# Output projection of a conv and pool hybrid layer: six products in token chunks of 512, 512 and 8 in place of three of 344

## What is computed

```python
def trunk(x, c, conv_bufs, pool_bufs, start, w_ada, b_ada, g_norm, w_in, w_dw, b_dw,
          ln_g, ln_b, w_a_out, w_grp, pool_scale, w_b_out, w_out, g_final):
...
        m = jax.nn.sigmoid(proj[..., o5:o6]) * y_a + jax.nn.sigmoid(proj[..., o6:]) * y_b
        x = x + gate * (m @ w_out[l])
...
    return rms_norm(x, g_final), jnp.stack(new_conv), jnp.stack(new_pool)
```

## Time and profile before

| | |
|---|---|
| median of three executions | 1007.66 us |
| span of the profiled execution (first to last instruction) | 1007.2 us |
| TensorE busy in it | 977.5 us, 97% |
| VectorE busy in it | 694.8 us, 69% |
| ScalarE busy in it | 253.0 us, 25% |
| mean granted TensorE clock | 0.992 of full speed |

### The profile page before, as it was taken

How to read it: one execution, slowest core, us unless ns; L and a number is a source line. 1 busy time by engine, 2 the same in 40 slices (tenths; PEclk the granted TensorE clock), 3 DMA queues, 4 the chain that set the end, 5 groups by cost and what they waited for, 6 DMA issues and landing times.

```text
span 1007.2 us, 14744 instructions
## 1 busy us (share of the span) xinstructions
PE 977.5 (97%) x6196; PEld 962.9 (96%) x6196; DVE 694.8 (69%) x687; ACT 253.0 (25%) x264; POOL 1.9 (0%) x12
## 2 busy tenths in 40 slices
PE   4999999999999989999998999999999999999997
PEld 3799999999999979999998999999999998999996
DVE  6878987718898752889864489987879744343346
ACT  5541112121111221111211111122724512122241
POOL 0000000000000000000000000000000000000000
PEclk9999999999999999999999999999999999999998
DMA  9511221231230240122024112213871173124104
GB/s 379 234 43 63 93 72 53 84 121 42 84 116 27 74 143 22 63 84 96 27 75 142 42 42 106 79 53 106 331 283 40 40 315 126 42 85 189 42 1 169
DMA packets 31965, 106.46 MB, mean 106 GB/s; under 512 B 7713, under 2 KB 14113, under 8 KB 28449
## 3 DMA queue, kind: packets, MB, share of 16 engines
q1 hardware_dynamic: 28304, 92.82, 25.4%
q10 hardware_dynamic: 3600, 12.72, 3.2%
HBM read 82.74 MB, written 22.79 MB: 105 GB/s over the span
## 4 chain that ended last, share of the span: by engine, by line
PE 96%; DVE 1%; DMA 1%; issue 1%; ACT 1%; SPq 0%; DVEq 0%
PE ps L463 31%; PE ps L464 31%; PE ps L466 31%; DMA bf<-x_t 1%; PE aux L415 1%; DVE stage_hi L888 1%; PE ps L428 1%; PE aux L449 1%; PE aux L421 0%; PE aux L637 0%; DVE hf L1161 0%; ACT hf L712 0%; PE aux L629 0%; DVE bf L902 0%; ACT bf L706 0%
## 5 line engine op out<-in xcount | busy, mean ns | idle before, releaser
L464 PE MATMUL ps<-hr,w_hi 128*128 128x344 f32 x1536 | 488.3, 321 | 6.8 <-issue 6.8
L463 PE MATMUL ps<-hr,w_hi 128*128 128x344 f32 x1344 | 427.9, 321 | 2.2 <-ACT stage_hi L754 1.2
L930 DVE SCALAR_TENSOR_TENSOR conv_y<-conv_u,par,conv_y 128x1024 f32<-128x1024 f32 x240 | 308.1, 1284 | 20.6 <-PE ps L466 14.1
L464 PEld LDWEIGHTS ps<-hr,w_hi 128*128 128x128 f32 x1536 | 290.0, 189 | 7.3 <-issue 7.3
L466 PE MATMUL ps<-hr,w_lo 128*128 128x344 f32 x1344 | 286.0, 321 | 0.0
L463 PEld LDWEIGHTS ps<-hr,w_hi 128*128 128x128 f32 x1344 | 253.7, 189 | 4.5 <-issue 2.9
L466 PEld LDWEIGHTS ps<-hr,w_lo 128*128 128x128 f32 x1344 | 225.9, 189 | 0.0
L680 ACT ACTIVATE w_hi<-w_raw 128x1024 fp32r<-128x1024 f32 (+1 forms) x88 | 87.6, 996 | 274.3 <-PE ps L466 263.2
L864 DVE TENSOR_TENSOR w_lo<-w_raw,w_hi 128x1024 fp32r<-128x1024 f32 (+1 forms) x88 | 101.2, 1150 | 52.0 <-ACT w_hi L680 46.7
L463 PE MATMUL ps<-gr,w_hi 128*128 128x344 f32 x384 | 123.3, 323 | 0.0
L464 PE MATMUL ps<-gr,w_hi 128*128 128x344 f32 x384 | 121.8, 320 | 0.0
(11 more groups left out here) (128 smaller groups left out, 593.8 us busy)
## 6 DMA issues: line engine op xcount, KB each, us to landing
w_raw<-w_main SPq DMA_DIRECT2D x80, 512.0 KB, 3.3
ada_raw<-w_ada SPq DMA_DIRECT2D x8, 1024.0 KB, 16.8
bf<-x_t SPq DMA_DIRECT2D x4, 1032.0 KB, 8.0
sig_a<-stage_lo ACTq DMA_DIRECT2D x8, 516.0 KB, 2.7
sig_b<-stage_hi ACTq DMA_DIRECT2D x8, 516.0 KB, 2.6
y_conv<-conv_y SPq DMA_DIRECT2D x8, 516.0 KB, 3.0
silu_z<-stage_hi ACTq DMA_DIRECT2D x8, 516.0 KB, 4.0
bf<-y_conv SPq DMA_DIRECT2D x4, 1032.0 KB, 6.9
```

Of the source, the lines that this page charges most:

```text
L463: nc.tensor.matmul(out, wh, rhs_hi[:, cols(c)], start=(k == 0), stop=False)
L464: nc.tensor.matmul(out, wh, rhs_lo[:, cols(c)], start=False, stop=False)
L930: return v.scalar_tensor_tensor(out=y, in0=conv_u[:, x, k:k + SEQ], scalar=par[:, x, k:k + 1], in1=y, op0=ALU.mult, op1=ALU.add)
```

## The change

The first six products of the output projection are made by a new function, `wide_product`. Their token chunks are 512, 512 and 8 columns in place of three of 344, in the same three PSUM banks. The number of matmuls in a k step stays nine, and the columns that they stream stay 1032 in each of the three passes. The hardware loop of `job_pairs` is gone for these six. Since the first 1024 columns now fill two whole banks, VectorE makes the new x of the prompt in one instruction over both banks (`wide_x`) in place of three. The last two products and all that is before JOB_OUT are as they were.

```diff
+BANK = 512
+WIDE = [(0, 0, BANK), (1, BANK, SEQ), (2, SEQ, TOK)]
...
-            single(JOB_OUT, m_hi, m_lo, before_k=lambda k: pe.wait_ge(m_lo_done, k + 1))
-            job_pairs(JOB_OUT + 1, 4, m_hi, m_lo)
-            single(JOB_OUT + 5, m_hi, m_lo)
+
+            def wide_product(s):
+                pe.wait_ge(w_lo_done, s + 1)
+                pe.wait_ge(dve_evac, PAIRS * DVE_EVACS + s - 1 - JOB_B)
+                for k in range(KT):
+                    if s == JOB_OUT:
+                        pe.wait_ge(m_lo_done, k + 1)
+                    wh = w_hi[:, s % 2, k * P:(k + 1) * P]
+                    wl = w_lo[:, s % 2, k * P:(k + 1) * P]
+                    for bank, t0, t1 in WIDE:
+                        out = ps[:, s % 2, bank, 0:t1 - t0]
+                        nc.tensor.matmul(out, wh, m_hi[k][:, t0:t1], start=(k == 0), stop=False)
+                        nc.tensor.matmul(out, wh, m_lo[k][:, t0:t1], start=False, stop=False)
+                    for bank, t0, t1 in WIDE:
+                        last = nc.tensor.matmul(ps[:, s % 2, bank, 0:t1 - t0], wl, m_hi[k][:, t0:t1], start=False, stop=(k == KT - 1))
+                last.then_inc(pe_done, 1)
+
+            for s in range(JOB_OUT, JOB_OUT + 6):
+                wide_product(s)
...
+            def wide_x(m):
+                gate = mod[:, 4 + m // 4, m % 4, :]
+                product = ps[:, (JOB_OUT + m) % 2, :, :].rearrange("p c t -> p (c t)")
+                v.scalar_tensor_tensor(out=hf[:, KT + m, 0:SEQ], in0=product[:, 0:SEQ], scalar=gate[:, 0:1], in1=hf[:, m, 0:SEQ],
+                                       op0=ALU.mult, op1=ALU.add)
+                xs = hf[:, KT + m, SEQ:TOK]
+                link(v.tensor_tensor(xs, product[:, SEQ:TOK], gate[:, 1:NMOD], ALU.mult))
+                return v.tensor_tensor(xs, xs, hf[:, m, SEQ:TOK], ALU.add)
...
-                link(new_x(m, 0, CHUNKS))
+                link(wide_x(m))
```

## The result

The changed kernel takes 1021.03 us (median of 4 executions, 1020.29 to 1023.32), the kernel before 1007.73 (median of 4). The ratio is 1.0143 with a 95% interval of 1.0123 to 1.0162, so the change costs 14.4 us, between 12.4 and 16.3; the two medians lie 13.3 us apart. The forecast was 1021, with a range of 1014 to 1025.

What follows compares the result with a forecast made beforehand. TensorE's matmul stream was taken as the bound: a k step of 6 x 227.8 + 3 x 111 = 1700 ns in place of 1420, over 48 k steps +13.4 us on 1007.66, so 1021 us, range 1014 to 1025.

Steps and rivals of the forecast that it cites:

- What bounds the kernel: In the six products TensorE's stream never waits, so any nanosecond it gains or loses there is the kernel's; stretch 68.15 us.
- The short ones: Each 8-column matmul of the six products takes as long as its weight load, 111 ns, range 76 to 121.
- sign of being wrong: In the six products, records behind an 8-column matmul starting less than 70 ns apart, or doubled short matmuls, would refute the prediction.
- The long ones: Each 512-column matmul of the six products takes 227.8 ns, with 14.4 ns fixed per matmul; range 213.3 to 234.8.
- The loop, VectorE, the waits: In the six products, loop removal worth nothing, semaphore waits the same, VectorE's saving of 0.2 to 0.3 us a product hidden.
- Fully hidden loads: Rival: in the six products short matmuls cost only their columns, giving 1007.7 or 1001.4 us; 5% together with the skill's rule.
- A load at one cycle a column: Rival: fp32r weights in the six products load faster, a short matmul 67.7 ns, +7.2 us, 1014.9 us; 10%.
- Doubled short matmuls: Rival: each 8-column fp32r matmul of the six products runs as two, 222 ns, +29.4 us, 1037 us; 5%.
- The clock stayed at 1.00: Against the rival that the granted clock falls to 1.2 GHz in the six products, 1080 us or more; 2%.

Runs made afterwards that it cites:

- left out: Changed kernel without its 8-column matmuls, but for two in each product: 1005.47 us, ratio 1.000 to the kernel before.
- 120-column chunk: Changed kernel with chunks of 512, 400 and 120 columns in place of 512, 512 and 8: 1013.92 us, ratio 1.0077 to the kernel before.
- joined: Changed kernel with high by high and high by low of the sample columns as one 16-column matmul, VectorE adding the two: 1015.82 us, ratio 1.0110.
- three more: Changed kernel with low weights by the 8 sample columns run four times in place of once in each k step: 1037.54 us in one execution.
- grouped half weights: Changed kernel with the three 8-column matmuls of a k step in a row, most taking 64 of 128 weight columns: 1015.34 us, ratio 1.0098.
- half-weight runs: Changed kernel with most 8-column matmuls taking 64 of 128 weight columns: 1020.87 us, and 1015.34 us with the three of a k step in a row.
- written-out products alone: Changed kernel's code without the hardware loop, chunks put back to three of 344 and the new x in three instructions: 1005.33 us, ratio 0.9998.
- short ones apart: Changed kernel with the nine matmuls reordered so that each 8-column one stands between two of 512 columns: 1020.75 us, ratio 1.0133.
- the run above: Changed kernel with chunks of 512, 280 and 240 columns and the new x in three instructions: 1005.92 us, ratio 0.9995 to the kernel before.

## Why the prediction was right

**What bounds the kernel.** Right: TensorE's stream is the path in either kernel, and the 14.8 us by which the six products grew lie within the 12.4 to 16.3 us by which the kernel did.

**The short ones.** I took 111 ns from the fp32 rows of 9 and 128 columns, and from load records of equal length for fp32 and fp32r. The runs gave 111 to 112 ns in four ways (left out, 120-column chunk, joined, three more), and the grouped half weights 54 ns for each load of half the columns. The Trainium skill, in "TensorE: Matmul & The Clock Gate", section "LDWEIGHTS (loading the stationary operand)", gives columns / 1.2 in ns, 107 ns for 128, and the runs agree with some 4 ns beside it. One thing in the prediction's picture was loose. It said that only 8 columns stand over the next load to hide it, which is right, and then that a short matmul takes as long as its weight load. It is the successor's load, which only the half-weight runs could show, since in the changed kernel all loads are alike.

The prediction also gave a sign of being wrong: records behind an 8-column matmul that start less than 70 ns apart. By the starts of the matmul records that sign is there, 0.03 us. It was put on the wrong record: the record of a matmul can start ahead of its weights and is then longer. By the starts of the loads and by the products the price is 0.11 us, so the sign, taken as it was meant, did not appear.

**The long ones.** The step that was mis-sized. The prediction took 14.4 ns as a fixed cost of each matmul, since weights change once per matmul, and so 227.8 ns at 512 columns. Measured: 232.6. Of the 14.4 ns at 344 columns some 10 grow with the columns; only 4.7 are fixed. The short fp32 matmuls were a hint, with 107 + 4 ns and not 107 + 14, though no run shows that these 4 ns and the 4.7 are the same thing. The reason that was given, one change of weights per matmul, can account for no more than the 4.7 ns. The term is 6 x 48 x 4.8 ns = 1.4 us, and with it the sum is 13.4 + 1.4 = 14.8 us, what the stretch grew by.

That the forecast of 1021 met the median of 1021.03 to the last digit is luck. The sum was 1.4 us short, the medians lie 13.3 us apart while the stretch grew by 14.8, and single executions of the kernel before spread from 1004.1 to 1009.9 us, the longest at the lowest mean granted clock, 0.991.

**The loop, VectorE, the waits.** Right: the written-out products alone change nothing. The new instruction takes 1.28 us, within 1.2 to 1.3, TensorE had no wait in the stretch, and the stretch behind it takes 24.86 us where some 24.8 were forecast.

**The rivals.** Fully hidden loads fell with the short ones apart (1020.75 us). The Trainium skill, in "TensorE: Matmul & The Clock Gate", section "Back-to-back issue gap", gives about 25 ns from one matmul to the next at 1 to 64 columns, for an isolated gap. On fp32r, with a weight load for each, the measured price is 111 ns; on bf16 the rule is about right, with 0.03 us. A load at one cycle a column, 67.7 ns for a short matmul, fell with the 111 ns. Doubled short matmuls did not appear: there are 6196 matmul records in both profiles. The clock stayed at 1.00 in the stretch.

## What to carry to other kernels

A matmul that loads its own weights covers the load of the matmul behind it only while it streams. On fp32r at a granted clock of 1.00 that takes some 240 columns for 128 weight columns, by (111 - 4.7) / 0.445 = 239; 240 columns cost nothing extra in the run above. Below that a matmul costs 111 ns however few columns it has: 8 and 120 were measured. So when a width does not divide by the largest chunk, cut it evenly: a remainder of 8 columns costs as much as one of 240, while larger chunks in themselves win next to nothing, here 4.7 ns for each matmul saved, by the fitted line. A price per instruction that is read at one width should be split into its fixed part and its part per column before it is carried to another width, with whatever short rows the trace has.

## What was not expected

A column on fp32r costs 0.445 ns at a granted clock of 1.00, 7% over one cycle of 2.4 GHz. With bf16 operands, read at a stride of four bytes, it would be (225 - 4.7) / 512 = 0.43 ns, if the fixed part is the same. Fresh starts in PSUM, zero weights and a busier VectorE leave it as it is. What sets it stays open; how the moving operand is read from SBUF was not tried.
